# A hybrid decoder layer with routed experts on one core: the first half's rows reach the router by block transposes and DMA instead of by TensorE

## The reference, cut to what matters

```python
x = x + g1 * mixed                                 # after three token mixers
h2 = rms_norm(x, norm2_g) * (1 + sc2) + sh2        # the normalised rows
g_logits = h2 @ w_router_g + b_router_g            # (rows, 4)
e_logits = h2 @ w_router_e + b_router_e            # (rows, 32)
# top-1 group, top-2 experts in it; their SwiGLU experts on h2, weighted, added to x
```

## Time and profile before

| What | Value |
|---|---|
| median of 3 runs | 1568.68 us (1566.61 to 1568.91) |
| the profiled execution, its own time | 1566.17 us |
| its span | 1564.4 us |
| TensorE busy | 1525.1 us (97%) |
| VectorE busy | 1243.4 us (79%) |
| ScalarE busy | 799.9 us (51%) |
| GpSimd busy | 385.6 us (25%) |
| mean rate of the DMA engines | 232 GB/s |

### The profile page before, as it was taken

The page is one execution under the profiler, slowest core; times in us unless marked ns, Lnnn a source line. Parts: engine busy times, 40 slices in busy tenths (PEclk is TensorE's granted clock), DMA queues, the critical chain, the costliest instruction groups (busy, mean ns, idle before and its releaser), DMA issues.

```text
span 1564.4 us, 24156 instructions
## 1 busy us (share of the span) xinstructions
PE 1525.1 (97%) x9496; PEld 1325.1 (85%) x9496; DVE 1243.4 (79%) x1728; ACT 799.9 (51%) x886; POOL 385.6 (25%) x316
## 2 busy tenths in 40 slices
PE   6999999999999999999999999999999999999995
PEld 5888888878889999999999995888888888888883
DVE  4668887766747988896765548999999999999996
ACT  4222332335333213323342346877888778887775
POOL 0353000000000000001100202247656554444531
PEclk9999999999999999999999999999999999999997
DMA  9976322425434322232423477999999999999976
GB/s 335 327 215 209 89 81 84 153 81 151 126 90 149 122 81 84 73 96 85 130 80 94 143 268 293 399 406 403 396 394 404 406 390 378 384 390 391 390 271 249
DMA packets 220850, 363.33 MB, mean 232 GB/s; under 512 B 20358, under 2 KB 169934, under 8 KB 195640
## 3 DMA queue, kind: packets, MB, share of 16 engines
q1 hardware_dynamic: 196906, 323.19, 56.8%
q0 software_dynamic: 23184, 36.43, 8.0%
q10 hardware_dynamic: 646, 2.15, 0.4%
HBM read 363.01 MB, written 32.08 MB: 253 GB/s over the span
## 4 chain that ended last, share of the span: by engine, by line
PE 88%; DVE 5%; SPq 3%; DMA 1%; issue 1%; DVEq 1%; ACT 1%; POOL 0%; POOLq 0%; ACTq 0%
PE z L3174 16%; PE z L3176 16%; PE z L3175 16%; PE z L971 7%; PE z L969 7%; PE z L970 7%; PE z L986 4%; PE z L988 4%; PE z L987 3%; PE q L3062 2%; PE q L958 2%; DVE wl L1407 1%; SPq L1741 1%; PE q L977 1%; PE q L3088 1%
## 5 line engine op out<-in xcount | busy, mean ns | idle before, releaser
L1407 DVE TENSOR_TENSOR wl<-wr,whr 128x2048 fp32r<-128x2048 f32 x190 | 428.4, 2283 | 0.0
L3174 PE MATMUL z<-h_hi,w_hi 128*128 128x272 f32 (+1 forms) x1232 | 400.0, 325 | 0.0
L3176 PE MATMUL z<-h_hi,w_lo 128*128 128x272 f32 (+1 forms) x1232 | 396.6, 322 | 0.0
L3175 PE MATMUL z<-h_lo,w_hi 128*128 128x272 f32 (+1 forms) x1232 | 395.4, 321 | 0.0
L733 ACT ACTIVATE whr<-wr 128x2048 fp32r<-128x2048 f32 x190 | 360.0, 1911 | 54.0 <-PE z L971 50.9
L2329 DVE TENSOR_TENSOR w_lo<-w_raw,w_hi 128x1024 fp32r<-128x1024 f32 (+1 forms) x169 | 179.5, 1063 | 120.2 <-ACT w_hi L2020 120.1
L3174 PEld LDWEIGHTS z<-h_hi,w_hi 128*128 128x128 f32 x1232 | 231.8, 188 | 19.7 <-issue 3.6
L3176 PEld LDWEIGHTS z<-h_hi,w_lo 128*128 128x128 f32 x1232 | 231.6, 188 | 15.9
L3175 PEld LDWEIGHTS z<-h_lo,w_hi 128*128 128x128 f32 x1232 | 231.9, 188 | 14.9
L2518 DVE SCALAR_TENSOR_TENSOR conv<-a_in,parT,conv 128x512 f32<-128x512 f32 x360 | 193.7, 581 | 13.8 <-issue 0.4
L969 PE MATMUL z<-whr,xTh 128*128 128x512 f32 x512 | 202.7, 396 | 0.0
(11 more groups left out here) (547 smaller groups left out, 2343.4 us busy)
## 6 DMA issues: line engine op xcount, KB each, us to landing
wr<-in_w_dram SPq DMA_DIRECT2D x198, 1024.0 KB, 10.7
w_raw<-in_w_in_dram SPq DMA_DIRECT2D x104, 512.0 KB, 3.8
w_raw<-in_w_branch_dram SPq DMA_DIRECT2D x48, 256.0 KB, 2.7
ada<-in_w_ada_dram SPq DMA_DIRECT2D x5, 2048.0 KB, 12.4
w_raw<-in_w_out_dram SPq DMA_DIRECT2D x16, 512.0 KB, 4.1
ada_h<-in_w_ada_dram SPq DMA_DIRECT2D x2, 2048.0 KB, 15.0
ada_u<-in_w_ada_dram SPq DMA_DIRECT2D x2, 2048.0 KB, 10.8
ada_m<-in_w_ada_dram SPq DMA_DIRECT2D x2, 2048.0 KB, 11.7
```

Source lines behind the costliest of these rows:

```text
L1407: return dve.tensor_tensor(out, a, b, op)
L3174: pe.matmul(out, w_hi[w][:, k, :], hi[:, k, t0:t1], start=(k == 0), stop=False)
L3175: pe.matmul(out, w_hi[w][:, k, :], lo[:, k, t0:t1], start=False, stop=False)
L3176: last = pe.matmul(out, w_lo[w][:, k, :], hi[:, k, t0:t1], start=False, stop=(k == kn - 1))
```

## The change: what it does

The eight TensorE transposes of each first-half tile and ScalarE's copy of them are gone. In their place:

- VectorE transposes the 32x32 blocks of each normalised tile into h2b right after the add, one instruction of 128x1024 per tile, with a drain ahead of it. `h2_ok` now counts this instruction. h2b lies over vT and gq, gt and cv, the two ot tiles, and a scratch tile.
- GpSimd writes h2b to memory beside h2s (four more transfers of 512 KB), waits for all eight, and then reads h2T back with 32 transfers, each of 32 partitions by 16 runs of 32 elements (128 bytes).
- `first_columns` waits for these and runs after stage B's second chunk, `first_rows` after its third. ScalarE's `scores_read(0)` moves to ahead of B's chunk 2 and VectorE's `first_scores` to after B's last chunk. LT moves to the place of chb.
- Waits on h2_out count eight stores instead of four, and VectorE gets one, in `c_chunk(0)` ahead of its first write to cv.

```diff
+        h2b_dram = nc.dram_tensor("h2_blocks", (HALF, D), F32, kind="Internal").ap()
+        BLK = 32
+        h2b = [at(f"h2b{t}", [P, D], F32, o)[0] for t, o in enumerate((vT_at, gt_at, ot_at))] + [h2s[PT]]
+        h2t_in = (h2_out, 32 * PT)
@@ GpSimd
                 pool.dma_start(h2_dram[t * P:(t + 1) * P, :], h2s[t][:]).then_inc(h2_out, 16)
+                pool.dma_start(h2b_dram[t * P:(t + 1) * P, :], h2b[t][:]).then_inc(h2_out, 16)
+            def blocks_in():
+                blocks = h2b_dram.rearrange("(a c) (k b u) -> b k c a u", c=BLK, k=KD, u=BLK)
+                for k in range(KD):
+                    for b in range(P // BLK):
+                        pool.dma_start(h2T[BLK * b:BLK * b + BLK, k, :].rearrange("c (a u) -> c a u", u=BLK), blocks[b, k]
+                                       ).then_inc(h2t_in[0], 16)
                     for t in range(PT):
                         tail_out(t)
+                    pool.wait_ge(h2_out, 32 * PT)
+                    blocks_in()
@@ ScalarE
-                    if g and i:
-                        tail_tile(i - 1)
-                        if g and i == 0 and k == 1:
-                            tail_tile(PT - 1)
-                                act.wait_ge(h2_out, 16 * PT)
+                                act.wait_ge(h2_out, 32 * PT)
-                            if g and i == 0:
-                                scores_read(0)
                 for i in range(CW):
+                    if g and i == 2:
+                        scores_read(0)
                     b_chunk(i)
@@ VectorE
-                tt(h, h, B2[:], ALU.add).then_inc(h2_ok, 1)
+                tt(h, h, B2[:], ALU.add)
+                dve.drain()
+                dve.transpose(h2b[t][:], h).then_inc(h2_ok, 1)
-                    if g and i == 1:
-                        first_scores()
+                    if g and i == 0:
+                        dve.wait_ge(h2_out, 32 * PT)
                 for i in range(CW):
                     b_chunk(i, 3, (1, 2))
+                if g:
+                    first_scores()
@@ TensorE
-                    if g:
-                        if i:
-                            h2_transpose(i - 1)
-                    if g and 1 <= i <= 3:
-                        (lambda: h2_transpose(PT - 1), first_columns, first_rows)[i - 1]()
+                pe.wait_ge(h2t_in[0], h2t_in[1] + 16 * KD * P // BLK)
                 for i in range(CW):
                     v_chunk(i)
+                    if g and 1 <= i <= 2:
+                        (first_columns, first_rows)[i - 1]()
```

More of the change, by code:

```diff
@@ L179, in build @@
         sig = sb("sig", [P, TM])
+        chb_at = top[0]
         chb = sb("chb", [P, TM])
@@ L237, in build @@
         assert o_lt <= act1_end
-        LT[0], _ = at("LT0", [P, HALF], F32, vT_at)
+        LT[0], _ = at("LT0", [P, HALF], F32, chb_at)
         A2, o = at("A2", [P, D], F32, h_at + 5 * 4 * 4 * FF)
@@ L547, in build @@
             if g:
-                for i in range(PT):
-                    use(0, "h2T", 0, i)
+                pass
             for i in range(CW):
@@ L691, in dense_done @@
             eng.wait_ge(he_ok, PT + 1 - NH_D)
-            eng.wait_ge(h2_out, 16 * PT)
+            eng.wait_ge(h2_out, 32 * PT)
             eng.wait_ge(lg_rd, 2)
@@ L838, in moe_gpsimd @@
             dense_done(pool)
-            pool.wait_ge(h2_out, 16 * (PT + 1))
+            pool.wait_ge(h2_out, 16 * (2 * PT + KD * P // BLK + 1))
             def fill_table(t):
@@ L1977, in _ @@
                         tail_out(t)
+                    pool.wait_ge(h2_out, 32 * PT)
+                    blocks_in()
             pool.wait_ge(first_tok_ok[0], first_tok_ok[1] + 1)
-            pool.wait_ge(h2_out, 16 * PT)
+            pool.wait_ge(h2_out, 32 * PT)
             pool.indirect_dma_start(first_x[:], None, h2_dram[0:HALF, :], bass.IndirectOffsetOnAxis(ap=first_tok[0:XR, 0:1], axis=0),
@@ L2089, in chunk_squares @@
                                    accum_out=sp8[0:rows, t, c:c + 1]).then_inc(x1_sq, 1)
[L2091 to L2095, removed]
             def scores_read(g):
@@ L3228, in second_item @@
                 last.then_inc(item_mm, 1)
[L3230 to L3235, removed]
             def column_scores(out, x, c, first, last):
@@ L3248, in first_columns @@
                 pe.wait_ge(par2_in, 16 * N_PAR2)
-                q_wait_read(pe, "h2T", 0, PT - 1)
-                q_wait_free(pe, "vT", 1, 0)
+                pe.wait_ge(h2t_in[0], h2t_in[1] + 16 * KD * P // BLK)
+                q_wait_read(pe, "oT", 0, KD - 1)
                 for c in range(KD):
@@ L3368, in _ @@
                         second_item()
-                    if g:
-                        if i:
-                            h2_transpose(i - 1)
-                    else:
+                    if g == 0:
                         (parameters, histories, lambda: mod_columns(4), lambda: mod_columns(5))[i]()
```

## The result

The changed kernel takes 1573.82 us (median of 6 runs, 1572.36 to 1577.04) against 1567.60 us for the kernel before (median of 6 runs, 1566.30 to 1568.91): ratio 1.004, 95% interval 1.003 to 1.0051. It is 0.4% slower. The profiled execution took 1572.36 us with a span of 1570.6, that is 6.2 us over the profiled execution of before, by its own time and by its span. The forecast was +4.6 us. The direction, the place and most of the size were right; 1.6 us are missing from the sum. The forecast time itself, 1573.3, is only 0.5 us from the measured median, and that nearness is partly luck: with six runs the median of the kernel before is 1567.60, 1.1 us under the 1568.68 of the three runs that I had added my sum to, and this hides most of what the sum lacks.

What follows compares the result with a forecast made beforehand. TensorE, busy 97% of the span, bounds the kernel, with VectorE a close second in stages A and C. Transposes -3.5 and TensorE's waits on VectorE +8.1 give +4.6 us on 1568.68: 1573.3 us, range 1569.0 to 1579.0.

Steps and rivals of the forecast that it cites:

- TensorE's transposes, -3.5: Four groups of transposes, 0.87 us each, leave TensorE's chain of waits: -3.5 us.
- VectorE's transposes, 1.32 each: Each tile's VectorE transpose with its drain takes 1.32 us, like the add: 5.3 us over four tiles, between 4.2 and 10.2.
- The two-pass rival: VectorE's fp32 transpose needs two passes and costs 2.5 us: +9.5 us, 1578.2; chance 0.10.
- The three waits: TensorE waits for VectorE before items 7, 9 and 12 in stages A and C: 2.3, 2.1 and 3.1 us.
- The rival that TensorE's queue covers VectorE's delay: VectorE drops behind in stages A and C, TensorE stays the bound and gains 3.5 us: 1565.2; chance 0.12.
- Nothing is caught up: TensorE leaves stage C when it did before, within 0.1 us.: At stage C's end, TensorE's waits on VectorE have eaten the 8.1 us of transposes and products that left it.
- one of the things that I said would show me wrong: In stage C, the last chunk's cv<-z,cv coming over 1 us earlier or later than before, at 604.3.
- The moved products, 4.6 us: Router and row products come back in stage B on a chain that is TensorE's alone: 3.58 + 0.19 + 0.81 = 4.6 us.
- Stores, reads, GpSimd: Last stores land by 539.1 us, 1.7 of reserve; the 32 reads land by 570, 54 us of reserve: no cost.
- No price for VectorE: GpSimd's issuing of DMA does not slow VectorE: taps beside a store took 751 ns against 749.
- the late reads: Rival: landings do not overlap, TensorE stands still 31 us after item 23: 1604 us; chance 0.04.
- The reserve rival: The transpose is cheap or some unseen reserve exists: delay under 3.1 us, about 1570; chance 0.20.

Runs made afterwards that it cites:

- e3: Changed kernel with 12 wide-convolution taps moved from VectorE's stage A to the gate stage behind stage B; 1564.06 us against 1566.93 before.
- e2: Kernel before plus only VectorE's four transposes, their stores and waits; TensorE's transposes and products stay, nothing read back; 1569.02 us against 1566.93.
- e5: Changed kernel plus six unread matmuls on TensorE after item 11, to fill its wait; 1574.37 us against 1568.04 before.
- e7: Changed kernel with all 32 reads of the blocks issued twice, the waits counting 64; 1574.03 us against 1568.04 before.
- e9: Changed kernel plus three unread matmuls on TensorE after item 11, to fill its wait; 1573.08 us against 1567.04 before.
- e6: Changed kernel with every VectorE transpose done twice into the same tile; 1578.08 us against 1568.04 before.
- e8: Changed kernel with 6 taps moved from VectorE's stage A to the gate stage; 1567.03 us against 1568.04 before.
- e1: Kernel before with only the router products, scores_read and first_scores moved to stage B, transposes staying on TensorE; 1566.81 us against 1566.93.
- e10: Changed kernel run once more without further edits, beside the run with three unread matmuls; 1574.04 us, ratio 1.0044 to the kernel before.

## Why the prediction came out as it did

*TensorE's transposes, -3.5.* Right as what leaves TensorE. As a gain the runs show most of it and not all: e3 is faster by 2.9 us by the medians, 2.2 by the profiles and 2.5 in the trace of this stretch, with 0.4 us of waiting listed.

*VectorE's transposes, 1.32 each.* Right: 1.34. The two-pass rival is out: 1245 ns is the time of one pass of that shape (1226 for the add), not of two.

*The three waits.* Right in place, and nearly in time (a fourth, 0.2 us before item 5, was missing): a_in of chunks 2 and 3 ended at 514.55 and 528.69 (forecast 514.65 and 528.79), cv<-z,cv of the first C chunk at 550.57 (550.03). The rival that TensorE's queue covers VectorE's delay is out.

*"Nothing is caught up: TensorE leaves stage C when it did before, within 0.1 us."* This is the step that was mis-sized: 1.6 us instead of 0.1. It was also one of the things that I said would show me wrong (the last cv<-z,cv over 1 us off), and it did. Its terms, from VectorE's rows after against those forecast:
- the first cv<-z,cv 0.54 later: the 0.43 us pause before 541.51, marked as issue, and 0.27 for the copies and the first write to cv, slower beside the reads (the same cv<-z,cv starts at 549.58 in e2, which has the pause and no reads), less 0.16 by which VectorE was early there. The pause stands at the first instruction behind the new wait on h2_out, but the last store had landed before 539.7, so that it is not the landing. It stands there in the runs of the changed kernel, in e2, e5, e7 and e9. In e6 none was found in this stretch; in e3 one like it stands at 548.30, and in e8 one of 0.35 at 591.95. All kernels, the one before too, have another of 0.44 to 0.47 between 490.3 and 491.3. What makes them was not found.
- the pause of 0.83 before p_in of the second chunk: TensorE reached the end of item 12 some 1.5 us later than at the full clock, and would otherwise have been done 0.7 before VectorE needed it. This is the low clock. I had worked out the 3.1 us wait and stopped there: the sum held what the wait costs and not what the restart behind it costs.
- 0.18 in the two rounds of the loop after it (605.89 - 569.15 = 36.74 against 604.26 - 567.70 = 36.56 us).

Together 1.6, and +4.6 + 1.6 = +6.2, the profiled difference. Of this, e9 shows the clock's part in the trace: 1.1 of the 1.64 us go with it and 0.54 stay. The 0.54 is read off the rows and was not varied.

*The moved products, 4.6 us.* Right: 4.7 in stage B. e1 shows that moving them costs nothing while VectorE can use the room that they leave in stage C.

*Stores, reads, GpSimd.* Right in their times, and e7 puts the late reads out of the question. "No price for VectorE" was read from taps beside a store and holds for them; for the copies and one-input operations beside the reads it does not, which is 0.27 us here.

*The reserve rival* (under 3.1 us, about 1570) had its chance from reserves that I might not see. With both parts of the change there was none: e6 passes 4.7 of its 5.3 us of second transposes on. Where the products stay in stage C, as in e2, the pause of 4.97 us is such a reserve and only 2 of 5.3 us arrive.

## What to carry to other kernels

Work that leaves the bounding engine is worth its time only where the next engine is not already as late; before moving work from one to the other, give the receiver room, by moving its own deferrable work to a stage where it idles (here 12 taps, worth nothing alone, turned +0.4% into -0.2%). Two edits that cost 0 and 2 us alone can cost 6 together: here the first takes TensorE's work out of a stretch where the second leaves VectorE as the later engine, so that nothing fills TensorE's wait. And where a sum puts a wait of some microseconds in front of TensorE, it should also hold a stretch of matmuls behind it at the low clock, if what waits for those matmuls has no reserve.

## What the runs showed of the hardware

- After waits of 3.2 to 4.2 us TensorE's clock fell to 1.2 GHz each time one was looked at (changed kernel and e10 at item 12; e6 at items 7 and 12; e7 at item 12). After waits of 1.8 us it fell in e5 and e7 at item 7 and in e8 at item 12, and did not in the changed kernel, e9 and e10 at items 7 and 9. The low stretch began between 0.6 us before and 1.5 us after the first matmul behind the wait, and lasted some 3.4 us each time.
- It costs only where nobody else is later. In e7 the low clock after item 7's wait shortened item 9's wait:

```profile
514.80 0.36 PE L3184 MATMUL z<-h_hi,w_hi 128*128 128x272 f32 x1 [1.82 <-DVE a_in L2335]
...
528.94 0.36 PE L3184 MATMUL z<-h_hi,w_hi 128*128 128x272 f32 x1 [0.30 <-DVE a_in L2335]
```

  The second is 1.8 in the changed kernel, and item 9 starts when a_in is there in both.
- VectorE's transpose of the 32x32 blocks of 128x1024 fp32 took 1245 ns, about as long as an add of that shape (1226). On TensorE eight fp32 transposes of 128x128 took 0.87 us back to back.
- A GpSimd-issued read of 512 runs of 128 bytes took 0.65 us to issue and 2.8 us (median) to land; with 64 of them, from 539.8 to 588.5 us, both medians stayed (e7).
- Beside the issue of such reads VectorE's copies and one-input operations took 0.1 to 0.2 us longer each (0.27 against 0.17, 0.84 against 0.64; changed kernel against e2), while its taps kept their 749 ns.
